# A projection of 512 x 1024 by 1024 x 1024 as seven products of quarters, inside a two-layer kernel

## The reference, cut to what matters

```
h = rmsnorm(x, norm_pre)
proj = jnp.einsum('bld,de->ble', h, w_in)
z_ssd, xbc, dt_raw, q, k, v, z_sb, gates = jnp.split(proj, _split_points(), axis=-1)
...
y = ssd_scan(xs, dt, a, bm, cm, d_skip)
y = gated_group_rmsnorm(y, z_ssd, ssd_norm, SSD_GROUPS)   # y * silu(z_ssd), normed, * ssd_norm
y_ssd = jnp.einsum('ble,ed->bld', y, w_ssd_proj)
```

## Time and profile before

| | us |
|---|---|
| median of 3 runs | 1339.85 (1339.65 to 1340.01) |
| the profiled execution | 1333.97 |
| its span, first to last instruction | 1332.2 |
| PE busy in it | 1313.8 |
| DVE, ACT, POOL busy in it | 896.0, 684.6, 141.0 |

### The profile page before, as it was taken

The page is one execution under the profiler, slowest core; times in us unless marked ns, Lnnn a source line. Parts: engine busy times, 40 slices in busy tenths (PEclk is TensorE's granted clock), DMA queues, the critical chain, the costliest instruction groups (busy, mean ns, idle before and its releaser), DMA issues. The chain is left out here.

```text
span 1332.2 us, 19859 instructions
## 1 busy us (share of the span) xinstructions
PE 1313.8 (99%) x7533; PEld 1117.5 (84%) x7533; DVE 896.0 (67%) x1433; ACT 684.6 (51%) x1263; POOL 141.0 (11%) x166
## 2 busy tenths in 40 slices
PE   9999999999999999999999999999999999999998
PEld 7888888887877788888788878888889998999896
DVE  5786653458888844433738977657759887786777
ACT  6454442458778744323535466664335663554453
POOL 0015312101111001111010012112000000000000
PEclk9999999999999999999999999999999999999999
DMA  4223116965856458989252178877633555555554
GB/s 172 80 80 95 64 64 165 248 171 149 180 156 133 127 209 249 210 244 215 84 191 70 64 163 185 170 151 136 213 111 108 190 188 193 190 190 189 183 168 166
DMA packets 60448, 210.20 MB, mean 158 GB/s; under 512 B 6724, under 2 KB 8132, under 8 KB 60098
## 3 DMA queue, kind: packets, MB, share of 16 engines
q1 hardware_dynamic: 41602, 142.86, 32.7%
q0 software_dynamic: 18176, 65.02, 23.4%
q10 hardware_dynamic: 576, 1.05, 0.3%
HBM read 201.57 MB, written 69.21 MB: 203 GB/s over the span
## 5 line engine op out<-in xcount | busy, mean ns | idle before, releaser
L1657 ACT ACTIVATE whi<-wraw 128x1024 fp32r<-128x1024 f32 (+1 forms) x184 | 190.4, 1049 | 196.0 <-PE bank L1198 101.1
L1198 PE MATMUL bank<-a_hi,whi 128*128 128x512 f32 (+1 forms) x800 | 290.2, 363 | 0.5 <-DVE a_lo L2710 0.5
L1198 PE MATMUL bank<-a_hi,wlo 128*128 128x512 f32 (+1 forms) x800 | 280.1, 350 | 0.0
L1198 PE MATMUL bank<-a_lo,whi 128*128 128x512 f32 (+1 forms) x800 | 279.3, 349 | 0.0
L2088 DVE TENSOR_TENSOR wlo<-wraw,whi 128x1024 fp32r<-128x1024 f32 (+1 forms) x184 | 223.0, 1223 | 83.3 <-ACT whi L1657 79.9
L1198 PEld LDWEIGHTS bank<-a_hi,wlo 128*128 128x128 f32 x800 | 151.2, 189 | 20.6
L1198 PEld LDWEIGHTS bank<-a_hi,whi 128*128 128x128 f32 x800 | 151.9, 190 | 19.1 <-issue 2.3
L1198 PEld LDWEIGHTS bank<-a_lo,whi 128*128 128x128 f32 x800 | 151.7, 190 | 18.7 <-issue 1.7
L1198 PE MATMUL bank<-arena 128*128 128x128 f32 (+6 forms) x1012 | 139.4, 288 | 2.7 <-DVE arena L2701 1.1
L1198 PEld LDWEIGHTS bank<-arena 128*128 128x128 f32 (+1 forms) x1012 | 124.0, 190 | 12.4 <-issue 5.3
L1198 PE MATMUL bank<-whi,a_hi 128*128 128x512 f32 x288 | 115.0, 399 | 1.5 <-DVE wlo L2088 0.7
(11 more groups left out here) (303 smaller groups left out, 2323.6 us busy)
## 6 DMA issues: line engine op xcount, KB each, us to landing
wraw<-in_wblk SPq DMA_DIRECT2D x128, 512.0 KB, 4.7
wide_sums<-in_wides POOLq DMA_DIRECT2D x60, 512.0 KB, 8.2
sums<-in_quarters POOLq DMA_DIRECT2D x30, 512.0 KB, 7.2
arena<-wide_sums SPq DMA_DIRECT2D x21, 512.0 KB, 4.4
wide_sums<-wide_sums POOLq DMA_DIRECT2D x20, 512.0 KB, 5.7
wraw<-wide_sums SPq DMA_DIRECT2D x19, 512.0 KB, 4.7
wraw<-in_wides SPq DMA_DIRECT2D x17, 512.0 KB, 4.6
arena<-in_wides SPq DMA_DIRECT2D x13, 512.0 KB, 4.7
```

Source lines behind the costliest of these rows:

```text
L1198: return nc.tensor.matmul(o, lhsT, rhs, start=start, stop=stop, **kw)
L1657: A(whi[n % 2][:, cols], tile, ACT.Copy).then_inc(s_hi, 1)
```

## The change

z's four blocks are replaced by seven, one for each product (`z_products`), with 4 chunks and 2 tiles of 128 tokens each: 8 parts in 8 slices. With quarters a11 to a22 of the input (first digit: tokens, second: features) and b11 to b22 of the weights, the order is a11 b11, a12 b21, s2 t2, s1 t1, s3 t3, s4 b22, a22 t4. Where it can be, a product goes on in the bank of the one before it, after ACT has copied that bank out (`z_held`); DVE adds or subtracts the others onto the copies, ACT takes the silu of two tiles at once (`z_silu`), and DVE gates y (`z_gate`). The sums of the input are made at z's first slices; s3 is made on POOL, right after its part of the scan. They lie where `b_hi` and `b_lo` are free. z has four raw buffers. The weight sums of z are two new chains ahead of all others, issued beside xbc, k and q; in z itself every fifth slice issues a transfer of the later chains. The row of y's norm is loaded once block 21's weights (the first of v) are split. The norm of y begins 5 slices into v.

```diff
+Z_BANKS = {1: (1, 2), 6: (1, 2), 7: (1, 2), 4: (1, 2), 2: (3, 0), 5: (4, 5), 3: (4, 5)}
...
+    def z_products():
+        for p in PRODUCT_ORDER:
+            gs = [tile({2: "z_late", 7: "z_add", 3: "z_add"}.get(p, "z"), (p, t)) for t in range(2)]
+            parts = [(t, k, whole[0]) for k in range(NK // 2) for t in range(2)]
+            blocks.append(dict(w="w_in", form="zprod", spans=[(0, 512)], k0=0, kn=NK // 2, tiles=gs, srcs=["A"] * 2, parts=parts,
+                               kb=0, total=NK // 2, closing=True, product=p))
+            yield p, [("gemm", len(blocks) - 1, sl) for sl in range(SLICES)]
...
-    for half in range(2):
-        steps += token("w_in", Z0 + 512 * half, "z", half, "A")
+    z_flow, z_events = [], {}
+    steps.append(("asum", "z", "s3"))
+    for at, x in zip((0, 3, 6, 10, 18, 22, 26), (("asum", "s1"), ("asum", "s2"), ("asplit", "s2"), ("asplit", "s1"),
+                                                 ("asplit", "s3"), ("asum", "s4"), ("asplit", "s4"))):
+        z_events[at] = [(x[0], "z", x[1])]
+    for p, made in z_products():
+        z_flow += made
+        e = len(z_flow) - 1
+        if p in QUADRANT_OF:
+            if p == 2:
+                z_events[e + 14] = [("zadd", p)]
+            if p != 4:
+                z_events.setdefault(e + (16 if p == 2 else 4), []).append(("zsilu", QUADRANT_OF[p]))
+            z_events.setdefault(e + (19 if p == 2 else 6), []).append(("zgate", QUADRANT_OF[p]))
+    for i, step in enumerate(z_flow):
+        steps += [step] + z_events.pop(i, [])
...
-    steps += weave(sum(ys, []), vs[:24]) + vs[24:28] + [("stack",)] + vs[28:]
+    steps += vs[:5] + weave(sum(ys, []), vs[5:28]) + [("stack",)] + vs[28:]
...
-SUM_CHAINS = GATE_UP(range(4)) + ...
+SUM_CHAINS = [("z", i) for i in range(2)] + GATE_UP(range(4)) + ...
...
-    times = into("z")[::3] + into("v")[:16:3] + ...
+    z = [s for s in STEPS if s[0] == "gemm" and BLOCKS[s[1]]["form"] == "zprod"]
+    first = (into("xbc") + into("k") + into("q"))
+    times = first[8:40:6] + first[40:100:6] + z[::5] + into("v")[:16:3] + ...
...
+def raw_slots():
+    slots, users = {}, {}
+    for n, b in enumerate(BLOCKS):
+        for i in range(2):
+            far = (n - Z_START) % 2 if b["form"] == "zprod" or n == Z_START + len(PRODUCT_ORDER) else (n - FF0) % 2 if n >= FF0 else 0
+            of = users.setdefault(2 * far + i, [])
+            slots[n, i] = 2 * far + i, len(of) + 1, of[-1] if of else None
+            of.append((n, i))
+    return slots
...
+                    elif n == Z_START + 1:
+                        sp.wait_ge(*((s_yd, 4 * (NT - 1)) if i else (s_st, 2 * (NT - 1))))
+                    elif before is not None:
+                        sp.wait_ge(s_lo, 2 * before[0] + i + 1)
...
-                if n == block_of("z") + 3:
-                    sp.wait_ge(s_yd, 4 * NT)
-                    sp.wait_ge(s_xd, 2 * NT)
+                if n == Z_START + len(PRODUCT_ORDER) + 1:
+                    sp.wait_ge(s_lo, 2 * n)
                     sp.dma_start(rows["y"], dram["ssd_norm"]).then_inc(s_row["y"], 16)
...
+                if TILES[g][0] == "z" and BANK[g] >= 4:
+                    pe.wait_ge(s_y, NT)
...
+                if kind == "z":
+                    p, t = i
+                    act.wait_ge(s_y, NT)
+                    if p == 4:
+                        A(z_last[:, t, :], ps[:, :], ACT.Silu).then_inc(s_end["S"], 1)
+                    else:
+                        A(z_held[KEEPS[p]][:, t, :], ps[:, :], ACT.Copy).then_inc(s_end["S"], 1)
...
+                    if i == (0, 0):
+                        act.wait_ge(s_yz, 2 * NT)
                     A(vt[:, t, 512 * half:512 * half + 512], ps[:, :], ACT.Copy).then_inc(s_end["S"], 1)
...
+            def z_silu(quadrant):
+                p = next(p for p, x in QUADRANT_OF.items() if x == quadrant)
+                act.wait_ge(*ended(tile_of("z_late" if p == 2 else "z_add", (p, 1))))
+                r = z_held[HELD_IN[quadrant]]
+                A(r, r, ACT.Silu).then_inc(s_zg, 1)
...
+                if kind in ("z_add", "z_late"):
+                    p, t = i
+                    r = z_held[HELD_IN[QUADRANT_OF[p]]][:, t, :]
+                    dve.wait_ge(s_tile, DONE[g])
...
+                    if p == 2:
+                        last = v.tensor_tensor(r, r, ps[:, :], ALU.add)
+                    elif p == 7:
+                        last = v.tensor_tensor(r, r, ps[:, :], ALU.subtract)
+                    else:
+                        last = v.tensor_tensor(r, ps[:, :], r, ALU.subtract)
...
+                if s == ON_POOL:
+                    dst = wide_part(z_f32, "s3")
+                    part = lambda of, x: f32(a_part(of, x))
+                    pool.wait_ge(s_split, max(SPLITS.index(x) for x in SPLITS if x[0] == "chunk") + 1)
+                    g_.tensor_tensor(dst, part(a_hi, "a11"), part(a_hi, "a21"), ALU.subtract).then_inc(s_zsum, 1)
+                    pool.wait_ge(s_zsum, 1)
+                    g_.tensor_tensor(dst, dst, part(a_lo, "a11"), ALU.add).then_inc(s_zsum, 1)
+                    pool.wait_ge(s_zsum, 2)
+                    g_.tensor_tensor(dst, dst, part(a_lo, "a21"), ALU.subtract).then_inc(s_zsum, 1)
```

More of the change, by code:

```diff
@@ L468, in plan_tiles @@
             ended += BLOCKS[s[1]]["tiles"]
+        elif s[0] == "zadd":
+            ended += [TILES.index(("z_late", (s[1], t))) for t in range(2)]
         elif s[0] == "evac":
@@ L512, in plan_tiles @@
             banks = (4 + 2 * PAIR[at[1]] + at[2],)
+        if kind in ("z", "z_add", "z_late"):
+            banks = (Z_BANKS[at[0]][at[1]],)
+        if (kind, at) == ("v", (0, 0)):
+            uses[banks] += 2
+        if (kind, at) == ("gate2", 0):
+            uses[banks] -= 2
         if kind in ("wide_s", "wide_v"):
@@ L618, in plan_splits @@
             order.append(s)
-            last["wide", s[1]] = len(order)
+            last["wide", s[1], s[2]] = len(order)
         if s[0] == "small":
@@ L628, in plan_splits @@
                     continue
-                if b["form"] == "wide":
-                    name = PRODUCTS_OF[b["products"][j][1]][0]
+                if b["form"] in ("wide", "zprod"):
+                    name = PRODUCTS_OF[b["product"] if b["form"] == "zprod" else b["products"][j][1]][0]
                     chunk = k % 4 + 4 * (name != "a11")
-                    need[s[1], j, k, 0] = last["wide", name] if name in WIDE_SUMS else max(last["A", t, chunk] for t in range(NT))
+                    need[s[1], j, k, 0] = last["wide", "z" if b["form"] == "zprod" else "ff", name] if name in WIDE_SUMS else max(last["A", t, chunk] for t in range(NT))
                     continue
@@ L677 @@
 LATE = min(n for n, b in enumerate(BLOCKS) if TILES[b["tiles"][0]][0] == "z_sb") + 1
-LOADED = [n for n, b in enumerate(BLOCKS) if b["form"] not in ("product", "wide")]
+LOADED = [n for n, b in enumerate(BLOCKS) if b["form"] not in ("product", "wide", "zprod")]
 NWIDE = (FFP[-1][1] - WIDE0) // 2
@@ L713, in sum_times @@
     units = [s for s in STEPS if s[0] == "nsa" and SPLIT_LAG < s[1]]
-    times = into("z")[::3] + into("v")[:16:3] + of("gate_ssd")[8::2] + of("gate_sb")[::2] + sum([[s, s] for s in units], [])
+    z = [s for s in STEPS if s[0] == "gemm" and BLOCKS[s[1]]["form"] == "zprod"]
+    first = (into("xbc") + into("k") + into("q"))
+    times = first[8:40:6] + first[40:100:6] + z[::5] + into("v")[:16:3] + of("gate_ssd")[8::2] + of("gate_sb")[::2] + sum([[s, s] for s in units], [])
     out = {}
@@ L1072, in half_block, with summed_input @@
             return of[i // 2][:, PIECE * (i % 2):PIECE * (i % 2) + PIECE]
+        asum_steps, asplit_steps = [[s[1:] for s in STEPS if s[0] == what and s != ON_POOL] for what in ("asum", "asplit")]
+        def summed_input(stage, name):
+            if ("asum", stage, name) == ON_POOL:
+                return s_zsum, 3
+            return s_asum, asum_steps.index((stage, name)) + 1
         def wide_bank(q, p):
@@ L1112, in weights_of @@
                 cols = piece(n, i)
+                if BLOCKS[n]["form"] == "zprod":
+                    name = PRODUCTS_OF[BLOCKS[n]["product"]][1]
+                    return (dram["z_quarters"][QUARTERS.index(name)] if name in QUARTERS else z_sums[SUMS.index(name)])[:, cols]
                 if BLOCKS[n]["form"] == "wide":
```

143 lines of the change are left out of this document (95 added, 48 removed).

## The result

The changed kernel takes 1341.88 us (median of 20 runs, 1338.89 to 1345.15); the kernel before took 1339.26 beside it (20 runs, 1333.64 to 1341.81). The ratio is 1.0024, 95% interval [1.0014, 1.0033]: slower by 2.6 us, beyond 0.2%. Predicted were 1337.0 and a range to 1341.5.

The account below looks back on a forecast made before the run. PE's own instructions were taken to bound the kernel. Profiled: 1333.97 - 5.4 (fewer matmuls) + 2.6 (waits) = 1331.2 us; median: 1339.85 - 2.8 = 1337.0 us, with a range of 1334.4 to 1341.5.

Parts of the forecast that it names:

- the term for the 16 early transfers: Beside xbc, k and q: transfers summing z's quarters go through POOL's queue at a cost of 0, at most 1 us.
- The base: Whole kernel: the profiled run's 1333.97 us lies 5.9 below the median 1339.85; that difference is carried over unchanged.
- z's own sum: In z: 24 fewer matmuls save 5.4 us, PE's waits cost 2.6 with loads landing after 6.4 us; 2.8 gained.
- The walk for 9.3 us: In z: if loads land after 9.3 us, waits total 6.5 us, 1.1 us slower than before.
- rival B: In z: loads landing near 9 us stall PE 6.5 us, giving 1340.9 (from 1338.5 with 8 us); chance 0.18.
- the silu ahead of the rounding: In z, block 19: ACT's silu of product 2 precedes the rounding, making product 3's rest 1.0 to 1.9 us late.
- Rival C: In z: POOL's queue shares engines packet by packet, starving loads; v starts some 5 us later, 1345 us; chance 0.12.
- s3 on POOL: Before z: POOL's three operations lengthen some DVE scan operations by 0.9 us each; cost to PE 0, at most 1.
- The row of y's norm: At y's first turns in v: the row of weights, loaded later, costs 0, at most 2.4 us.
- rival D: At y's first turn: the norm's row comes late, 2 us of PE's wait above forecast, 1338 to 1340; chance 0.11.
- DVE full in z: In z: DVE has 39 us of work in a window of 38.1, leaving about 2 us of air.
- Rival A: In z: everything hides and the 5.4 us are gained, up to 1 lost, 1334.4 to 1335.5; chance 0.23.

Follow-up runs that it names:

- second profile: The kernel before, unchanged, profiled once more: 1340.48 us (one run), where the first profiled run took 1333.97 us.
- the last experiment: Changed kernel with all of POOL's transfers out of z, and s3 moved from POOL to DVE inside z: 1334.65 us, ratio 0.9979 to the kernel before.
- the repeat: Second timing of the changed kernel with 20 transfers beside k and q, 8 before the decays and none in z: 1332.94 us, ratio 0.9959.

## Why the prediction was wrong, point by point

**The step that failed** is the term for the 16 early transfers, put at "0, at most 1": "They go through POOL's queue ahead of its scan work; an issue takes about 0.7 us and a lane's turn comes every block ... 0, at most 1." It measured 4.3 to 5.1 us (after against the kernel that differs in their issue times alone) and 4.6 to 5.5 (against the kernel without them). What it looked at, the mean share of the DMA engines and the mean spacing, was not the question. The row with the 20% is of 150 to 193, and the loss came from transfers that left at 78 to 85. There too the share of before is low, 0.29 and 0.35. What it left out:
- POOL doesn't issue when the list says. The trace of before shows POOL idle until 77.84 for the decays (the row below). What stands behind them in the list waits with them, and leaves as soon as they and the lane allow.
- Who stands behind a load. The text asked whether POOL's own work would be late. The load was late, ACT's rounding behind it, and a tile's copy behind the rounding, though nothing in the copy needs weights.
- The clock. A wait was priced at its length; this one came with 2.3 us more at the lower clock.

```profile
77.84 3.10 POOL L2822 TENSOR_TENSOR b_hi<-b_hi,cst 128x512 fp32r<-128x512 f32 x3 [77.41 <-DVEq L2584]
```

With the transfers better timed the kernel is at 1336.7, and the forecast was 1337.0; but that nearness is partly chance, as the next points show.

**The base.** "It lies 5.9 below the median of the runs, and I carry the difference over." The difference was no constant. In the second profile it was the wait of 4.4 us in y and its clock, in the very stretch that the change rearranges, and after's profile doesn't have it: 0.28 us. Carrying it over left out a gain of about 6 us against most runs of before; without it the changed kernel would stand some 9 us behind them (an estimate: the 2.6 measured and the 6.2 of this place).

**z's own sum.** 5.4 us removed: right, shown by 24 fewer matmuls and by z's 38.4 us once loads land in 4 to 5. The waits were put at 2.6 and were 4.1 by name, 5.4 with all; the term that was mis-sized is the landing, 6.4 taken, 8.2 in z's median and 10.6 where the longest wait arose. The walk for 9.3 us, with 6.5 of waits, was the nearer one. So inside z it was **rival B** that came true. That its 1340.9 lies 1.0 from the measured time is luck: it had neither the 6.1 us ahead of z nor the gain in y. The place was right: some 30 us into z, at 245.13 (28.1 in). The reason named, the silu ahead of the rounding, is not enough: with quick loads nothing waits there.

**Rival C** forecast slower, and slower it was, by something else. It wanted v 5 us later because z's loads get too little; v came 6.1 later, but z was as long as before. The loads moved 2.45 MB from 230 to 245 in after, 163 GB/s, above its point of 144. Its idea that POOL's transfers take the engines from the loads was right in kind, in a stage where it was not looked for. For the share, the Trainium skill (DMA: Bandwidth & Descriptors, section "Queues, rings and completion order") has an engine take turns between queue rows by packets. No run here shows it or speaks against it: in after from 230 to 245 there were 382 packets of POOL's queue and 676 of the loads', but the counts don't tell when both had work. The 173 GB/s of before couldn't settle the shares for the same reason.

**s3 on POOL**: 0, at most 1; PE's wait beside it was 0.7 in after, where 1.0 was lost, and 1.2 in the kernels with no transfers in z. The Trainium skill (SBUF — State Buffer, section "SBUF: two separate sides") has the port pair that DVE and GpSimd share as a lock held for the whole instruction. The prediction weighed it against 0.9 us for each operation that meets POOL. The trace agrees: an operation that takes 0.69 took 2.88, a rest of 1.23 took 2.38, and in the kernels without transfers in z a rest took 3.93. Each is, within 0.2 us, its own length and what was left of the instruction of POOL that it met (of 2.39, 3.26 and 3.0 us). It can be more than one instruction: the 4.99 us of the last experiment stand beside three. My row of 1.55 had met one of 1.04 us only the earlier trace rows, so 0.9 for each was too little beside s3. The price for PE stayed small because PE had slack for most of it.

**The row of y's norm** (0, at most 2.4) and **rival D**: PE never waited for it; moving it changed nothing that the intervals can tell in either kernel. **DVE full in z**: right, as three operations more (3.7 us) turned into 2.9 us of waits. **Rival A**, everything hides: it is what z itself does, to 0.3 us (1.0 in the repeat), with no transfer of POOL in it, as in the late stage that the text named.

**A misreading** that changed nothing: 2.3 and 0.6 us are not PE's longest kinds of waits before. The view has 1.7, 1.4, 1.1, 1.1 and more between them.

The last test of the prediction was the one that spoke: "wrong altogether would be a wait that isn't in z or the first of v".

## What to carry to other kernels

A transfer that is cheap by the mean share of the engines can be dear when it leaves in a bunch: for each one added, look up what the issuing engine waits for just ahead of it, and which in-order engine has a load's consumer ahead of work that needs no load. When a profile is much quicker than the median of the runs, take a second profile before pricing anything: the difference was a wait in the stretch under change. Waits of PE of 2.5 us and more had a low clock behind them here: price a wait with it.

## What the runs showed that I had not expected

- PE's clock behind a wait. Over windows of 5 us it read 0.50 or 0.51 behind waits of 3.78, 4.37, 5.04 and 5.24 us, 0.70 behind one of 3.74, 0.66 behind one of 4.54 and beside ones of 3.81 and 2.94, and 0.76 beside one of 2.50; beside waits of 2.16, 1.77 and 1.47 us it stayed at 1.00. 0.50 is the level of 1.2 GHz, and each value between is a window with stretches at both levels. The Trainium skill (TensorE: Matmul & The Clock Gate, section "HAM oscillation — how this bites in real kernels") tells of a matmul kernel whose waits for loads throttle it again and again; here the work that was late was not a load but a tile.
- The kernel before has two forms: near 1335 without the wait in y, near 1339 with it. In the two profiles it hangs on one load, which landed after 4.5 us in the one and after 9.9 in the other. What decides it from run to run stays open; moving POOL's transfers out of z made 10 of 12 runs the quick one.
- Loads of 512 KB landed after 3.6 to 5.6 us in z when no transfer of POOL was issued there (medians 4.5 and 4.3 in two profiles), and after 5.7 to 11.1 us (median 8.2) in after's z beside POOL's DRAM-to-DRAM transfers.
